# Moving VectorE's short-convolution products, softmax steps and convolution taps to other slots of a hybrid decoder layer

## What is computed

```python
xn = rms_norm(x, norm_mix)
(sc_h, sc_b, sc_c, cf_a, cf_b, aq, ak, av, ...) = split(xn @ w_in)
conv_u = causal_dwconv(sc_c * sc_h, conv_short)          # width 3
o_a = sc_b * conv_u                                      # branch A: short convolution
c = causal_dwconv(cf_a * sigmoid(cf_b), conv_conf)       # branch B: width 31
o_c = sliding_window_attention(q, k, v, window=128)      # branch C: softmax in blocks of 128 queries
m = sum_r sigmoid(gate_r) * (branch_r @ w_branch[r])
x = x + m @ w_out ;  x = x + swiglu(rms_norm(x))
```

## Time and profile before

| quantity | value |
|---|---|
| runs: median, lowest, highest | 2051.53 us, 2046.03 us, 2051.7 us |
| the profiled execution: its time, its span | 2049.75 us, 2048.0 us |
| TensorE busy | 2012.5 us (98% of the span) |
| VectorE, ScalarE, GpSimd busy | 1231.0, 781.3, 380.1 us |
| mean granted TensorE clock | 0.995 of full speed |

### The profile page before, as it was taken

One profiled execution on the slowest core, in us unless ns is written; L12 is line 12 of the kernel. 1 busy time (PEld: TensorE's weight loads), 2 busy tenths in 40 slices (PEclk: granted clock), 3 DMA queues, 4 the chain that ended last, 5 costly groups with the idle time before them and its releaser, 6 DMA issues.

```text
span 2048.0 us, 38853 instructions
## 1 busy us (share of the span) xinstructions
PE 2012.5 (98%) x16572; PEld 1971.4 (96%) x16572; DVE 1231.0 (60%) x1667; ACT 781.3 (38%) x1209; POOL 380.1 (19%) x238
## 2 busy tenths in 40 slices
PE   7999999999999999999999999999999999999998
PEld 7999999999999999999999989999989999999998
DVE  5998678755546543355559876787455555533445
ACT  5314433653533342233233235346444333322332
POOL 0794000211103000000309920002111120000003
PEclk9999999999999999999999999999999999999999
DMA  7222222222322222222432221232223222222223
GB/s 263 80 103 76 71 93 83 83 96 83 124 84 103 94 86 93 98 83 79 142 124 93 89 81 63 94 104 86 73 102 126 83 104 82 92 93 93 93 77 129
DMA packets 38290, 199.51 MB, mean 97 GB/s; under 512 B 9298, under 2 KB 10450, under 8 KB 19664
## 3 DMA queue, kind: packets, MB, share of 16 engines
q1 hardware_dynamic: 29376, 180.03, 25.0%
q10 hardware_dynamic: 8784, 17.57, 2.5%
HBM read 187.42 MB, written 12.29 MB: 98 GB/s over the span
## 4 chain that ended last, share of the span: by engine, by line
PE 85%; DVE 11%; ACT 2%; issue 1%; DMA 0%; POOL 0%; ACTq 0%; DVEq 0%; POOLq 0%
PE acc L606 80%; DVE cacc L1320 2%; DVE wlo L1326 2%; DVE q L1317 1%; ACT tmp L987 1%; PE m L707 1%; PE m L694 1%; DVE sct L1320 1%; DVE gt L1317 1%; PE m L720 1%; PE m L623 1%; PE m L822 0%; PE m L794 0%; PE m L832 0%; PE m L782 0%
## 5 line engine op out<-in xcount | busy, mean ns | idle before, releaser
L606 PE MATMUL acc<-xhi,wlo 128*128 128x260 f32 x3680 | 753.9, 286 | 12.2 <-DVE xlo L1307 9.9
L606 PE MATMUL acc<-xhi,whi 128*128 128x260 f32 x3680 | 742.8, 283 | 0.0
L606 PE MATMUL acc<-xlo,whi 128*128 128x260 f32 x3680 | 742.0, 283 | 0.0
L606 PEld LDWEIGHTS acc<-xhi,wlo 128*128 128x128 f32 x3680 | 570.8, 189 | 26.4 <-DVE wlo L1293 9.8
L606 PEld LDWEIGHTS acc<-xhi,whi 128*128 128x128 f32 x3680 | 568.9, 189 | 0.0
L606 PEld LDWEIGHTS acc<-xlo,whi 128*128 128x128 f32 x3680 | 568.6, 189 | 0.0
L1326 DVE TENSOR_TENSOR wlo<-raw,whi 128x1024 fp32r<-128x1024 f32 (+3 forms) x344 | 436.7, 1278 | 36.3 <-ACT whi L1004 34.9
L1004 ACT ACTIVATE whi<-raw 128x1024 fp32r<-128x1024 f32 (+3 forms) x344 | 331.9, 994 | 238.6 <-PE acc L606 189.4
L987 ACT ACTIVATE gt<-gt 128x520 f32<-128x520 f32 x226 | 144.3, 639 | 212.1 <-DVE gt L1317 207.2
L1317 DVE TENSOR_TENSOR gt<-acc,rstd 128x520 f32<-128x520 f32 x80 | 55.8, 698 | 198.2 <-PE acc L606 185.9
L606 PE MATMUL acc<-hhi,whi 128*128 128x260 f32 x704 | 141.6, 282 | 0.0
(11 more groups left out here) (224 smaller groups left out, 2172.6 us busy)
## 6 DMA issues: line engine op xcount, KB each, us to landing
raw<-in_wt SPq DMA_DIRECT2D x142, 1024.0 KB, 4.8
raw<-in_wt SPq DMA_DIRECT2D x16, 768.0 KB, 4.0
raw<-in_wt SPq DMA_DIRECT2D x16, 640.0 KB, 3.7
x<-yt ACTq DMA_DIRECT2D x2, 2080.0 KB, 9.3
yt<-x ACTq DMA_DIRECT2D x16, 260.0 KB, 2.0
x<-in_xt SPq DMA_DIRECT2D x4, 520.0 KB, 6.9
yt<-in_xt SPq DMA_DIRECT2D x1, 2080.0 KB, 16.9
s<-in_gs ACTq DMA_DIRECT2D x4, 512.0 KB, 3.7
```

The source lines that it names most:

```text
L606: ins = nc.tensor.matmul(out[:, h], a, b[:, h * TH:h * TH + TH], start=first and n == 0, stop=last and n == 2)
```

## The change

Three things change in VectorE's program, and with the softmax steps also the slots of the attention's small work on TensorE and ScalarE. The products of the short convolution stand in the scb slot of their chunk, between taking scb out and the multiplication, instead of in the scc slot. Softmax steps 2 to 7 begin at slots 25, 27, 30, 32, 35 and 38. The taps of the wide convolution are spread otherwise over the slots; the last of the 93 stands in slot 53 as before.

```diff
-ATT = [S_AV + n for n in (7, 9, 11, 13, 19, 21, 24, 28)]
+ATT = [S_AV + n for n in (7, 9, 12, 14, 17, 19, 22, 25)]
...
-for _first, _last, _m in ((4, 7, 3), (8, 9, 4), (10, 17, 2), (20, 21, 2), (29, 29, 2), (30, 33, 1), (34, 37, 2),
-                          (38, 41, 1), (42, 53, 3)):
+for _first, _last, _m in ((4, 7, 3), (8, 9, 4), (10, 11, 2), (12, 15, 1), (20, 20, 2), (21, 21, 1), (22, 22, 2),
+                          (27, 27, 2), (29, 30, 2), (32, 32, 2), (34, 35, 2), (37, 38, 3), (40, 53, 3)):
...
                             st.need(tt(scu[:, c, W1 - 1:W1 - 1 + SEQ], tmp[:, c % 2, 0:SEQ], y[:, 0:SEQ], ALU.mult,
                                        "sc_written"))
 
+                        elif kind == "scb":
+                            y = sct[:, c % 2]
+                            out_of(n, tmp[:, c % 2])
+                            st.need(("sc_written", c + 1))
                             w = [par_("cs", c * W1 + i) for i in range(W1)]
                             for i in range(W1):
...
                             st.settled()
-                        elif kind == "scb":
-                            y = sct[:, c % 2]
-                            st.need(out_of(n, tmp[:, c % 2]))
+                            st.need(("acc_out", n + 1))
                             tt(y, y, tmp[:, c % 2], ALU.mult, "sc_o")
```

## The result

The changed kernel takes 2052.47 us (median of 12 runs, 2049.33 to 2055.27) and the kernel before, measured beside it, 2048.16 (12 runs, 2046.03 to 2051.9). The ratio is 1.0018, with an interval from 1.001 to 1.0025: by that ratio 3.7 us longer (the medians lie 4.3 apart). That lies within the range and within the 0.3% that the prediction called the same, but 7 us above the predicted time, and on the other side of the kernel before. The span of the profiled execution grew from 2048.0 to 2050.2 us.

A forecast was written before the change was run, and what follows sets the result against it. TensorE was taken as the bound, so reordering VectorE could pay only in TensorE's waits. The terms 0.9 + 1.7 + 1.6 + 4.0 - 2 x 1.8 = 4.6 us, off 2049.75, gave 2045.2 us, range 2039 to 2057.

The forecast's parts named there:

- The wait for `qz`: TensorE's wait behind product 17, 3.57 us in the first layer, was to go, with the fall of the clock.
- The 19.6 us: All that reordering can win from TensorE's waits and clock losses: 8.1 us in the first layer, 11.5 in the second.
- The new waits: TensorE was to wait 2.3 us behind product 19 and 2.7 behind product 20.
- Slot 24: TensorE's wait behind product 24 was to go, winning 1.6 us in the first layer and 4.0 in the second.
- The steps: Softmax steps 4 and 7 beside short slots: one more wait of 1.1 us, another 0.7 longer; 1.8 lost per layer.
- The six products: VectorE's short-convolution products in slots 18 and 19: 4.9 us together with taking the slot out.
- (c): Products in slots 24 and 25 hold up softmax step 2 beside GpSimd: 7.5 us per layer, 2060.2 us; chance 0.14.
- What becomes late next: Work behind the moved products in slots 18 and 19 becomes late; product 21 begins at 153.5, bounds 150.1 or 156.1.
- the 0.9 and 1.7 us: What product 21's earlier start was to keep of 5.4 and 6.4 us in the first and second layer.
- Rival (b): The clock falls at waits behind product 20 and perhaps 40, 1.7 us each per layer: 2052.0 us; chance 0.13.
- A third tap in slot 53: Wide-convolution tap on VectorE in slot 53, said to end where VectorE waited for ScalarE; no loss was counted.
- the sum: Whole kernel, both layers: 0.9 + 1.7 + 1.6 + 4.0 - 2 x 1.8 = 4.6 us less.

The follow-up runs named there:

- experiment 7: Changed kernel with decode probabilities and their copy earlier, softmax steps 4 to 7 off the short slots, wide-convolution taps out of slots 16 to 26: 2030.93 us.
- experiment 4: Changed kernel and kernel before, both with 29 of 30 tap pairs of GpSimd's fourth chunk left out: 2038.82 and 2031.37 us.
- experiment 2: Changed kernel with the decode probabilities one slot earlier and their copy in slot 19 ahead of the convolution's products: 2045.39 us.
- experiment 1: Parts of the change on the kernel before: products alone 2053.48 us, steps alone 2049.77, taps alone 2054.94, steps and taps 2053.75; the first is meant here.

## Why the prediction was wrong

**What was right.** The wait for `qz` went. The 19.6 us that reordering could win were sized well: experiment 7's profiled span is 2028.5 against 2048.0. The new waits came in the forecast places, and their sum, 3.52 + 1.69 = 5.2, is near the forecast 2.3 + 2.7 = 5.0. Slot 24 gave 2.0 and 4.25 (forecast 1.6 and 4.0). The steps cost 1.5 per layer (forecast 1.8). The six products took 139.86 - 135.35 = 4.5 and 150.60 - 145.60 = 5.0 with the taking out (forecast 4.9). Step 2 did not wait, so (c) did not happen.

**The step that failed is "What becomes late next"**: product 21 was to begin at 153.5, between the bounds of 150.1 and 156.1, and began at 156.5, outside them, though the six products took what was forecast. Of the 0.9 and 1.7 us that were to be kept, none was; the layers lost 2.1 and 0.7 instead. Two terms of that step were mis-sized, and both hang on GpSimd. From the multiplication to the end of the `split` I took 2.4 from rows 5; it measured 142.39 + 0.70 - 139.86 = 3.2, and 3.2 again in slot 19. The probabilities I took at 0.7; they measured 143.38 + 1.17 - 143.01 = 1.5. That is 0.8 + 0.8 + 0.8, which less 0.3 for the products is 2.1 of the 2.3 us by which the copy was late: it was there at 153.97 - 0.61 = 153.4 in place of 151.1. Experiment 4 shows the cause: without GpSimd's taps the multiplication takes 0.70 and the scaling 0.28, the wait for `sprob` is gone and that for `small` is 0.16. Experiment 2 shows what the lateness cost: with the probabilities and their copy ahead of this chain both waits go, and the span falls from 2050.2 to 2043.6 us. I had doubted the duration of the six products and taken those of the work behind them as fixed; what matters is which instruction happens to meet one of GpSimd's. The Trainium skill, "SBUF — State Buffer", section "Who interferes with whom", says that a VectorE instruction with two inputs in SBUF contends with a GpSimd instruction that reads SBUF. The traces agree for the gate multiplication: 1.83 us beside GpSimd, 0.70 without.

**Rival (b) came true as well**, in part. Product 21's start lost another 0.7 us in the first layer, since the products of `side(20)` took 3.1 us in place of 2.4, and its matmuls behind it 0.9 and 1.5 us in the two layers: 1.6 and 1.5, near the 1.7 that I had priced and left out. Behind product 40 the clock did not fall (1.00 from 276 to 284).

**A third tap in slot 53 was not free:** `gt` waits 0.52 us longer at slot 59 in each layer; in experiment 7, with two taps there, the waits for `gt` are 3.7 again as before.

In terms of the sum, over both layers: 5.4 us more at product 21's start, 2.4 for the clock behind it, 1.0 at slot 59, less 0.6 at slot 24 and 0.6 at the steps, make 7.6, and turn 4.6 us less into 3.0 more. The 2045.2 us were also counted from a profiled execution that held the fall of the clock at 485 us, 1.5 us that the changed kernel's did not have.

## What to carry to other kernels

When work is moved in a hand-written order, list what then stands behind it on its engine and which of that another engine waits for: here the change cost 3.7 us, and won 18 together with small instructions put ahead of the products, steps 4 to 7 away from the short slots, and taps out of the way of the steps. Price every instruction of such a chain at what it can take beside a busy GpSimd (here 1.83 us for a multiplication, 1.17 for a scaling), not at what it happened to take in one trace (1.07 and 0.34). And work that fills idle time of an engine costs nothing only if nothing awaited stands behind it.

## What was not expected of the hardware

A wait of 0.16 us, with 16 matmuls of 8 columns behind it, was followed by a half clock for some 3 us (experiment 4), and without it the same matmuls were not; but a wait of 0.46 us ahead of them left the clock at 1.00 (experiment 1), and at 485 us of the kernel before it fell without any wait. And nearly the same wait had two outcomes within one execution: in experiment 2 step 0 waited 2.69 us in the first layer and 2.67 in the second, and the windows behind them show

```profile
164.00:168.00 4.00, 3.86 (x34) 3.57 (x35) 3.93 (x6) 0.60 (x1) 3.82 (x3) 1.00 0.41 170
...
1177.00:1181.00 4.00, 4.00 (x26) 3.44 (x25) 3.93 (x7) 0.60 (x1) 3.82 (x3) 0.63 0.23 94
```

So the length of a wait alone does not tell whether the clock falls; in the changed kernel waits of 1.05 and 1.46 us left it at 1.00, and it fell behind those of 1.69 and 3.52. What decides in between stays open here. The Trainium skill, "TensorE: Matmul & The Clock Gate", section "HAM oscillation — how this bites in real kernels", speaks of gaps in which TensorE is idle. The fall behind 3.52 us agrees with it; those behind a gap of 0.16 us and behind none are not told by it.
